# A twelfth slot for the ring of gathered expert rows, in place of weights that are then loaded again for each chunk

## What is computed

```python
q = (xc @ wq).reshape(128, 8, 2, 128)                  # a chunk of 128 tokens
s = einsum('nhpd,hpkd->nhpk', q, subkeys)              # 2 x 128 scores for each head
...                                                    # top 16 of the sums of pairs: idx, gate g
act = gelu(einsum('nhkd,nd->nhk', u[idx], xc))
out = einsum('nhk,nhkd->nd', g * act, v[idx])
```

## Time and profile before

| | |
|---|---|
| median of three runs | 3047.15 us (3046.94 to 3048.32) |
| profiled execution, its own time | 3048.86 us |
| its span, first to last instruction | 3046.9 us |
| PE / DVE / ACT / POOL busy | 77% / 67% / 27% / 66% |
| gathers | 2048, 1084.36 MB on the queue of POOL, with their indices |
| other transfers, on the queue of SP | 77.54 MB |
| mean rate over the span | 382 GB/s; 419 in most of the 40 slices from 690 us on |

### The profile page before, as it was taken

One profiled execution on the slowest core, in us unless ns is written; L12 is line 12 of the kernel. 1 busy time (PEld: TensorE's weight loads), 2 busy tenths in 40 slices (PEclk: granted clock), 3 DMA queues, 4 the chain that ended last, 5 costly groups with the idle time before them and its releaser, 6 DMA issues.

```text
span 3046.9 us, 29321 instructions
## 1 busy us (share of the span) xinstructions
PE 2341.4 (77%) x9222; PEld 962.0 (32%) x9222; DVE 2046.8 (67%) x4621; ACT 807.5 (27%) x1928; POOL 2015.7 (66%) x2127
## 2 busy tenths in 40 slices
PE   6988997888787887778778878888777777533587
PEld 4855575323231342133222323133313322100011
DVE  3687698777676767767776776676776777566400
ACT  3567122222213321232122222322123212100122
POOL 3600155577777777777777777777777777777775
PEclk9989997897889778977898879978888789866799
DMA  9632499899999999999999999999999999999998
GB/s 348 209 150 76 160 338 386 359 413 419 419 419 419 418 414 419 416 409 419 419 413 409 419 418 417 412 411 419 418 404 419 419 419 418 416 420 415 418 420 343
DMA packets 335938, 1163.77 MB, mean 382 GB/s; under 512 B 40485, under 2 KB 51365, under 8 KB 333608
## 3 DMA queue, kind: packets, MB, share of 16 engines
q0 software_dynamic: 297792, 1084.36, 88.0%
q1 hardware_dynamic: 37994, 77.54, 7.0%
HBM read 1148.13 MB, written 13.63 MB: 381 GB/s over the span
## 4 chain that ended last, share of the span: by engine, by line
POOL 30%; DMA 27%; PE 19%; issue 12%; DVE 9%; ACT 3%; SPq 0%; DVEq 0%; POOLq 0%; ACTq 0%
POOL arena L615 30%; DMA arena<-in_v,arena 17%; DMA arena<-in_u,idx_u 9%; PE psum L2117 6%; DVE arena L1578 5%; PE psum L1916 2%; PE psum L2051 2%; PE psum L1796 2%; PE psum L1948 1%; PE psum L1963 1%; PE psum L1973 1%; PE psum L1937 1%; DMA arena<-in_w_mod 1%; DMA wbig<-in_w_mod 1%; DVE small L1414 1%
## 5 line engine op out<-in xcount | busy, mean ns | idle before, releaser
L1578 DVE CUSTOM_DVE_ANT_0 arena<-arena,psum 128x1024 f32<-128x1024 f32 x1024 | 1238.0, 1220 | 480.3 <-DMA arena<-in_u,idx_u 465.5
L2117 PE MATMUL psum<-arena 128*32 128x512 f32 x4096 | 1073.6, 719 | 439.0 <-DMA arena<-in_v,arena 427.9
L615 POOL DMA_INDIRECT arena<-in_u,idx_u x1024 | 963.0, 940 | 439.6 <-issue 250.1
L615 POOL DMA_INDIRECT arena<-in_v,arena x1024 | 974.7, 952 | 346.6 <-issue 279.7
L969 ACT ACTIVATE arena<-arena 128x32 f32<-128x32 f32 x1024 | 267.5, 313 | 1198.1 <-PE psum L2117 1197.7
L2117 PEld LDWEIGHTS psum<-arena 128*32 128x32 f32 x4096 | 187.8, 119 | 1246.5 <-issue 911.6
L2051 PE MATMUL psum<-wbig,arena 128*128 128x512 f32 x512 | 229.5, 601 | 1.1 <-ACT arena L931 1.1
L1916 PE MATMUL psum<-kT,arena 64*128 64x512 f32 (+1 forms) x384 | 206.2, 684 | 26.4 <-ACT arena L828 25.2
L1948 PE MATMUL psum<-v,arena 128*128 128x64 f32 x1120 | 160.0, 307 | 26.9 <-ACT arena L892 26.9
L1948 PEld LDWEIGHTS psum<-v,arena 128*128 128x128 f32 x1120 | 152.1, 219 | 40.4 <-ACT arena L892 39.0
L892 ACT ACTIVATE arena<-psum 128x512 f32<-128x512 f32 x168 | 88.2, 525 | 246.1 <-PE psum L1937 244.1
(11 more groups left out here) (268 smaller groups left out, 2092.3 us busy)
## 6 DMA issues: line engine op xcount, KB each, us to landing
arena<-in_u,idx_u POOLq DMA_INDIRECT x1024, 9.8
arena<-in_v,arena POOLq DMA_INDIRECT x1024, 10.0
arena<-in_w_mod POOLq DMA_DIRECT2D x20, 512.0 KB, 5.5
wbig<-in_wq SPq DMA_DIRECT2D x1, 7168.0 KB, 20.0
arena<-in_w_mod SPq DMA_DIRECT2D x12, 512.0 KB, 5.4
arena<-in_xin SPq DMA_DIRECT2D x5, 1024.0 KB, 9.5
arena<-in_w_mod SPq DMA_DIRECT2D x2, 2048.0 KB, 10.6
wbig<-in_w_mod SPq DMA_DIRECT2D x2, 2048.0 KB, 20.5
```

The costliest lines, as they stand in the source:

```text
L615: pool.indirect_dma_start(ring[:, r, :], None, t[table], bass.IndirectOffsetOnAxis(idx[:, j:j + 1], 0)).then_inc(got[r], 16)
L1578: V.tensor_tensor_reduce(ring[:, r, :], ring[:, r, :], hx_cur, 1.0, 0.0, ALU.mult, ALU.add, act_[:, j:j + 1]).then_inc(S["u_used"], 1)
L2117: ins = M(bank(4 + b)[QP * g:QP * g + QP, :], lhsT=sel[:, j % SELS, :], rhs=ring[:, r, 512 * b:512 * b + 512], start=(i == 0), stop=(i == ...
```

## The change

A twelfth ring buffer is placed where the first 1024 of 2048 columns of the last eighth of the query weights lie (`wq[:, 7, 0:1024]`, 4 KB for each of 128 partitions). Chunk 0 still computes its queries from there; the first gather into that place waits for its fourth `q_ready`. For each of the chunks 1 to 7 SP then loads these 512 KB into the memory of `lc` and `att`, after the chunk's output projection has read both, and two of the 32 query matmuls take their weights from there behind one new wait. The load of the next `lc` moves back until these two have run. Some semaphores are merged to make room for the new ones (`mod_turned`, `c_tanh_lam_exp`), which changes no order.

```diff
-RING = 11
+RING, ARENA_SLOTS = 12, 11
...
+        LC_AT = ATT_AT + 2 * KEYS + 4 * P
+        wq_last = arena[:, LC_AT:LC_AT + D]
...
-        ring = view(RING * D, RING, D)
+        ring = view(ARENA_SLOTS * D, ARENA_SLOTS, D)
...
+        def tile(r):
+            return ring[:, r, :] if r < ARENA_SLOTS else wq[:, KT - 1, 0:D]
...
             def load_l(n):
-                sp.wait_ge(S["out_half"], 2 * n)
+                wait(sp, "q_ready" if n > 1 else "out_half", 4 * n - 2 if n > 1 else 2)
                 sp.dma_start(lc, l_scr[:, :, n * P:n * P + P].rearrange("f p c -> p f c")).then_inc(S["l_loaded"], 16)
+
+            def load_wq_last(n):
+                sp.wait_ge(S["out_half"], 2 * n + 2)
+                sp.dma_start(wq_last, wqv[:, KT - 1, 0:D]).then_inc(S["wq_last_loaded"], 16)
...
             load_x(1)
+            load_wq_last(1)
             load_l(2)
             load_qz(2)
             load_x(2)
             for k in range(NX - 3):
+                load_wq_last(k + 2)
                 load_l(k + 3)
                 load_qz(k + 3)
                 store(k)
                 load_x(k + 3)
+            load_wq_last(NX - 1)
...
+                if c == 0 and j == ARENA_SLOTS:
+                    pool.wait_ge(S["q_ready"], 4)
                 freed(c, u_place(c, j))
                 gather("u", idx_u, j, slot(c, u_place(c, j)))
...
-                        ins = M(bank(i), lhsT=hxT[:, kt, :], rhs=wq[:, kt, 512 * i:512 * i + 512],
-                                start=(kt == 0), stop=(kt == KT - 1))
+                        w = wq[:, kt, 512 * i:512 * i + 512]
+                        if n and kt == KT - 1 and i < 2:
+                            if i == 0:
+                                pe.wait_ge(S["wq_last_loaded"], 16 * n)
+                            w = wq_last[:, 512 * i:512 * i + 512]
+                        ins = M(bank(i), lhsT=hxT[:, kt, :], rhs=w, start=(kt == 0), stop=(kt == KT - 1))
```

More of the change, by code:

```diff
@@ L331, in layer @@
             "gains_loaded", "wm_loaded0", "wm_loaded1", "wm_loaded2", "wm_loaded3", "wm_used",
-            "acc_loaded", "staged_in0", "staged_in1", "mod_summed", "mod_rows", "mod_out",
-            "silu_ready", "tanh_c", "g1_ready", "a2_ready", "b2_ready", "g2_ready",
-            "modT_ready", "kvl_loaded", "x_loaded", "x_sq",
+            "acc_loaded", "staged_in0", "staged_in1", "mod_summed", "mod_turned", "mod_out",
+            "silu_ready", "c_tanh_lam_exp", "g1_ready", "a2_ready", "b2_ready", "g2_ready",
+            "kvl_loaded", "x_loaded", "x_sq",
             "x_var", "x_sd", "xn_ready", "xT_first", "xT_ready", "hT_vec", "hT_act", "kv_ready", "lru_ready",
@@ L343, in layer @@
             "conv_done", "gates_r", "gates_i", "r_out", "i_out", "lru_a", "lru_m", "lru_i", "lru_s",
[L344 to L345 removed]
+            "lru_free", "lru_out", "lc_first", "lru_stored0", "lru_stored1", "z_sq", "z_tanh", "z_in", "z_done",
+            "wq_loaded", "wq_last_loaded", "wo_first", "wo_loaded", "g1_moved",
             "l_loaded", "xc_loaded", "scores_ready", "negmax_ready", "probs_ready", "sum_inverted",
@@ L614, in gather @@
             def gather(table, idx, j, r):
-                pool.indirect_dma_start(ring[:, r, :], None, t[table],
+                pool.indirect_dma_start(tile(r), None, t[table],
                                         bass.IndirectOffsetOnAxis(idx[:, j:j + 1], 0)).then_inc(got[r], 16)
@@ L687, in _ @@
             act.wait_ge(S["c_loaded"], 48)
-            A(csil, ccol, ACT.Tanh, scale=0.5).then_inc(S["tanh_c"], 1)
+            A(csil, ccol, ACT.Tanh, scale=0.5).then_inc(S["c_tanh_lam_exp"], 1)
             def x_norm(m):
@@ L810, in _ @@
             act.wait_ge(S["lam_ready"], 1)
-            A(lt[:, 1, :], lt[:, 0, :], ACT.Exp, scale=-1.0).then_inc(S["lam_exp"], 1)
+            A(lt[:, 1, :], lt[:, 0, :], ACT.Exp, scale=-1.0).then_inc(S["c_tanh_lam_exp"], 1)
             for m in range(1, NTOK // 2 - 1):
@@ L1130, in _ @@
             V = nc.vector
-            dve.wait_ge(S["tanh_c"], 1)
+            dve.wait_ge(S["c_tanh_lam_exp"], 1)
             dve.wait_ge(S["filled"], 2)
@@ L1324, in _ @@
             V.tensor_copy(rowm, bank(4)).then_inc(S["mod_cols"], 1)
-            dve.wait_ge(S["modT_ready"], 1)
+            dve.wait_ge(S["mod_turned"], 1)
             dve.wait_ge(S["acc_loaded"], 32)
@@ L1356, in _ @@
             ch.step(V.tensor_scalar(lb, lb, 0.5, None, ALU.mult))
-            dve.wait_ge(S["lam_exp"], 1)
+            dve.wait_ge(S["c_tanh_lam_exp"], 2)
             ch.link(V.tensor_scalar(lt[:, 2, :], lt[:, 1, :], 2.0, None, ALU.add))
@@ L1577, in u_slots @@
                     r = landed(dve, c, u_place(c, j))
-                    V.tensor_tensor_reduce(ring[:, r, :], ring[:, r, :], hx_cur, 1.0, 0.0, ALU.mult, ALU.add,
+                    V.tensor_tensor_reduce(tile(r), tile(r), hx_cur, 1.0, 0.0, ALU.mult, ALU.add,
                                            act_[:, j:j + 1]).then_inc(S["u_used"], 1)
@@ L1628, in _ @@
             negmax(0, 0)
-            dve.wait_ge(S["mod_rows"], 1)
+            dve.wait_ge(S["mod_turned"], 2)
             dve.wait_ge(S["gains_loaded"], 48)
@@ L1744, in mod_sum @@
                                 start=True, stop=True)
-                ins.then_inc(S["mod_rows"], 1)
+                ins.then_inc(S["mod_turned"], 1)
             def keys(m, tt):
@@ L1852, in _ @@
                 ins = T(bank(6)[:, j * P:(j + 1) * P], rowm[:, j * P:(j + 1) * P], ident[:, :])
-            ins.then_inc(S["modT_ready"], 1)
+            ins.then_inc(S["mod_turned"], 1)
             pe.wait_ge(S["kvl_loaded"], 16)
@@ L2117, in v_slots @@
                         ins = M(bank(4 + b)[QP * g:QP * g + QP, :], lhsT=sel[:, j % SELS, :],
-                                rhs=ring[:, r, 512 * b:512 * b + 512], start=(i == 0), stop=(i == QP - 1))
+                                rhs=tile(r)[:, 512 * b:512 * b + 512], start=(i == 0), stop=(i == QP - 1))
                     if j % 2:
```

## The result

The changed kernel takes 3056.61 us (median of 15 runs, 3053.98 to 3059.2). The kernel before, run beside it on the same chip, takes 3050.75 us (15 runs, 3046.44 to 3052.15). The ratio is 1.0019, with a 95% interval of 1.0012 to 1.0026: the change costs 5.8 us, between 3.7 and 7.9. The forecast was a gain of 2.5 us, and 3044.7 us with a range that ended at 3053.5. Part of the distance in absolute time isn't the change: the three runs that I started from, 3047.15 us, lie at the lower end of what the kernel before does, and their median is 3.6 us under that of all 15. The sign is wrong all the same.

What follows compares the result with a forecast made beforehand. The prediction took the DMA engines, at 420 GB/s, as the bound. Steady part: +7.5 for loads, -7.45 for shortages, taken as 0; chunk 0: -2.5 us; so 3047.15 became 3044.7 us, range 3039.5 to 3053.5 (8 in 10).

Steps and rivals of the forecast that it cites:

- The engines are the bound, at 420 GB/s.: Steady part, from 596 us to the last gather's issue: the 16 DMA engines, not POOL's pace, limit, with a 420 GB/s ceiling.
- Each of the eight places gives back what it lost, at most 1.25 us ... = 7.45 us: Steady part: at eight drops in rate the twelfth buffer recovers lost engine time, one gather at most each, together 7.45 us.
- The engines still have some eight gathers in line: Steady part: while POOL waits for a buffer, some eight gathers remain queued, from 9.9 us landing at 1.25 us each.
- Chunk 0, -1.25 for the twelfth gather in the still stretch.: Engines nearly idle from 585.5 to 596 us: one more gather is fetched there for nothing, -1.25 us.
- Chunk 0, -1.25 for one gather more behind the loads of `w_out`.: From 487 to 516 us: the DMA has one gather more behind it when the `w_out` loads slow the engines, -1.25 us.
- Six reloads in the steady part, +7.5; the first hidden.: Seven 512 KB weight loads: the still stretch absorbs the first, six delay later gathers by 1.25 us each, +7.5 us.
- TensorE's wait, the moved load of `lc`, the merged semaphores: 0.: The wait before the eighth query matmul, the later `lc` load and the merged semaphores each cost 0.
- rival 1: Steady part: reloads are paid and nothing comes back, +7.5 us; 3054.7 us, or 3053.4 with the free gather; chance 0.17.
- in all eight POOL's row of waits precedes: Argument against the no-gain rival: POOL waits before all eight steady-part drops, and its wait ends with a buffer.
- the landing rising from 9.9 towards 11: Sign of being right: a gather's landing time rises from 9.9 us towards 11, because the extra gather stands in line.
- Rival 2: Steady part: the thin loss of rate is the ring's too; net -6.6 us to 3040.5, or -12 to 3035; chance 0.14.
- rival 3: Whole kernel: POOL is the bound, loads cost nothing and 40 us of buffer waits could go, about 3005 us; chance 0.03.

Runs made afterwards that it cites:

- e2: The changed kernel with eleven slots instead of twelve, keeping the seven weight loads and the later load of `lc`; 3058.21 us, ratio 1.0026 to the kernel before.
- e11: The changed kernel with every load of weights done twice, the second after the first has landed; 3064.18 us, ratio 1.0047 to the kernel before.
- e12: The changed kernel with all waits, but each weight load bringing only 128 of 1024 columns; 3048.6 us, ratio 0.9997 to the kernel before.
- e10: The kernel before with gathered rows of 960 instead of 1024 numbers; 3015.61 us, ratio 0.9886 to the kernel before.
- e1: The changed kernel with its twelve slots but without the seven weight loads; 3048.73 us, ratio 0.9992 to the kernel before.
- e4: The changed kernel with thirteen slots instead of twelve and no weight loads; 3045.32 us, ratio 0.9981 to the kernel before.
- e9: Fifteen slots against the kernel before's eleven, four of them in the query weights, without weight loads; 3041.84 us, ratio 0.9969.
- e8: The kernel before with gathered rows of 960 instead of 1024 elements, on a slower chip; ratio 1.001 to the kernel before there.

## Why the prediction was wrong, point by point

- **The engines are the bound, at 420 GB/s.** Right in that e2, e11 and e12 cost their bytes at this rate. But the distance to POOL is thin (e10), and the line stands for one part of a gather in sixteen, not for all.
- **"Each of the eight places gives back what it lost, at most 1.25 us ... = 7.45 us".** This step failed. The steady part gave back 0.7 us in the kernel after, and 0.5 to 1.0 in the other kernels with more slots; e2, which has no slot more, shows 0.5 as well, so even this may not be the slot's (table). Two assumptions in it were wrong. The pause of POOL doesn't shorten by a gather, since with another slot the last part of each gather lands later by about a gather's length, and the sum on TensorE that ends the pause waits for it (3.06 us instead of 2.87 near 1905 us). And the drop in rate isn't mainly idleness that one gather fills: 5.1 of the 8.8 us are slow packets.
- **"The engines still have some eight gathers in line"**. Wrong: of the 9.9 us, 4.4 are what a landing takes at best, which leaves (9.9 - 4.4) / 1.25 = 4.4; by bytes, 3.2 on the mean were issued and not moved, since 9.9 us is the landing of the last part alone and half of the parts are there at 5.7. It went into the assumption that only the long pauses touch the engines.
- **Chunk 0, -1.25 for the twelfth gather in the still stretch.** Right: 140 gathers are out before the restart.
- **Chunk 0, -1.25 for one gather more behind the loads of `w_out`.** Right within what single profiles tell: from the first gather to the restart 1.1 us less in the kernel after, 1.7 in e1, 3.5 in e4 with two slots, 4.7 in e9 with four. The scatter is about half as large as one slot's effect (e2, with no slot more, is 0.6 less as well); the mean of the four kernels with twelve slots is 1.0 us under that of the two with eleven. VectorE's product 90 of 128 comes 168.9 us after the first gather before and 166.7 after.
- **Six reloads in the steady part, +7.5; the first hidden.** Right: +7.9 in e2, and 8.5 for six more in e11.
- **TensorE's wait, the moved load of `lc`, the merged semaphores: 0.** Right by the rows above and by e12. The eighth matmul comes at 566.6 and not at 561.0, since I had taken each record for a matmul; it leaves the load more time. The load of `lc` is issued 33 us behind the reload (574.53), not some 50.
- **The starting point.** The profiled kernel before reached its first gather at 358.3 us, the one after at 361.7, ahead of anything that the change touches. In e10, whose program up to there is that of before, it is 361.8: such a shift belongs to the single run, and it is 3.4 of the 7.9 us by which the two profiled spans differ. The rest is -1.1 to the restart and +5.5 behind it.

With this term at 0.7 instead of 7.45 the sum is -2.5 + 7.5 - 0.7 = +4.3 us, inside the measured 3.7 to 7.9. That is rival 1 with its free gather and the gain of chunk 0, at 0.17. What was held against it, "in all eight POOL's row of waits precedes", isn't so: at two of the eight places there is no wait beyond the usual one, as shown above. And where a wait does precede, the drop isn't as long as what is taken off the wait. One of the signs that the prediction named for its being right, the landing rising from 9.9 towards 11, came true (11.4) and was no sign of a gain: a longer line is just what swallows the slot. Rival 2 falls with e4 and e9 (417 GB/s with 13 and with 15 slots), rival 3 with e2, since reloads beside a bound POOL would have been free.

A version that beats the kernel before isn't in these runs. The free slots of e1, e4 and e9 leave out part of the query weights. A twelfth slot for chunk 0 alone, with one reload, should by the same sums give 2.4 - 1.25 = 1.2 us, less than can be measured here; it wasn't tried.

## What to carry to other kernels

Where the DMA engines are full, a deeper ring can go into the line alone, here into the line of one part in sixteen: look whether the landing time rises by the length of a transfer and whether the first fifteen parts land later too, and count a slot at what it prefetches in stretches in which the engines stand still, here 1.25 us at the restart and about as much in chunk 0, not at the producer's waits. What pays for the slot counts by its bytes, from whichever queue. And before forecasting a change of 0.1%, take the base from more than three runs.

## What was unexpected of the hardware

- With a ring of ten to fifteen buffers fifteen sixteenths of a gather land in 7.0 to 8.0 us at the median and the last sixteenth in 8.6 to 14.7.
- A drop in the rate to 320 GB/s leaves 14 and more packets under way in most of the stretch. Some 700 to 960 of the gathers' 244,000 packets of 4 KB take over 200 ns instead of 159, most of them 230 to 770.
- POOL's own step, 1.24 to 1.25 us a gather, and the engines' 1.25 us for its 512 KB lie so close that 6% fewer bytes gave 1.1% of the time.
- One chip ran the same program in 3412.5 us instead of 3050, with a mean granted clock of 0.78 instead of 0.86 in e8 and e10, and neither more slots nor fewer bytes made it faster there.
